# Softmax maxima negated bank by bank, and attention units passed in two rounds, in a four-layer macaron decoder

## The reference

```python
for l in range(4):
    h = h + 0.5 * swiglu(rms_norm(h), ffn1[l])          # 1024 -> 2816 -> 1024
    aq, ak, av, rq, rk, rv, rg = split(rms_norm(h) @ w_in[l])
    h = h + concat([attention(aq, ak, av, sinks[l]), retention(rq, rk, rv, rg)]) @ w_out[l]
    h = h + 0.5 * swiglu(rms_norm(h), ffn2[l])

def attention(q, k, v, sink):    # 8 query heads, 2 kv heads, 64 wide, window 128, blocks of 128
    s = q @ kk.T * 64 ** -0.5    # kk, vv: the block before and the block itself, 256 keys
    s = where(mask, s, -1e30)
    m = maximum(max(s), sink)
    p = exp(s - m)
    return (p / (sum(p) + exp(sink - m))) @ vv
```

## Time and profile before

| | us |
|---|---|
| median of 3 runs | 5002.9 (5000.14 to 5364.91) |
| the profiled execution, its own time | 4998.59 |
| span of its slowest core, and of all cores | 4997.0 (4987.1 to 4997.0) |
| TensorE matmul busy | 4824.5 (97%) |
| VectorE busy | 2432.0 (49%) |
| ScalarE busy | 1902.8 (38%) |
| GpSimd busy | 818.8 (16%) |
| mean granted TensorE clock | 0.991 of 2.4 GHz |

### The profile page before, as it was taken

How to read it: one execution, slowest core, us unless ns; L and a number is a source line. 1 busy time by engine, 2 the same in 40 slices (tenths; PEclk the granted TensorE clock), 3 DMA queues, 4 the chain that set the end, 5 groups by cost and what they waited for, 6 DMA issues and landing times.

```text
span 4997.0 us, 74942 instructions; the slowest of 8 cores (4987.1 to 4997.0 us)
## 1 busy us (share of the span) xinstructions
PE 4824.5 (97%) x24992; PEld 2229.8 (45%) x24992; DVE 2432.0 (49%) x4938; ACT 1902.8 (38%) x3615; POOL 818.8 (16%) x1150
## 2 busy tenths in 40 slices
PE   7998899999999999999999999999999999989898
PEld 3443444444444444444444444444444444444343
DVE  2265645454454545555454554545445454455532
ACT  2134533534234342433434343343432534263522
POOL 0121121210212112120210202102121210201121
PEclk9999999999999999999999999999999999999999
DMA  6444545464554545545445554545445354435255
GB/s 144 77 87 70 87 73 98 72 100 72 90 94 74 101 72 92 86 81 95 74 86 85 90 89 74 98 72 97 83 83 98 66 100 80 82 67 103 45 112 101
DMA packets 129032, 430.78 MB, mean 86 GB/s; under 512 B 14608, under 2 KB 14736, under 8 KB 128656
## 3 DMA queue, kind: packets, MB, share of 16 engines
q0 software_dynamic: 116640, 404.54, 47.5%
q1 hardware_dynamic: 12016, 21.45, 1.5%
HBM read 822.03 MB, written 8.39 MB: 166 GB/s over the span
## 4 chain that ended last, share of the span: by engine, by line
PE 88%; DVE 4%; ACT 4%; issue 2%; DMA 1%; POOL 1%; DVEq 0%; ACTq 0%; SPq 0%; POOLq 0%
PE pf L493 46%; PE pf L524 21%; PE pm L614 9%; PE pm L957 4%; PE pm L766 2%; DVE nF L427 1%; ACT scr L846 1%; PE pm L874 1%; PE pm L820 1%; PE pm L886 1%; ACT L846 1%; DVE pm L826 1%; PE pm L662 1%; DMA ringF<-w_gu 1%; DVE nM L427 0%
## 5 line engine op out<-in xcount | busy, mean ns | idle before, releaser
L493 PE MATMUL pf<-nF,ringF 128*128 128x512 bf16 x11264 | 2564.4, 382 | 15.6 <-DMA ringF<-w_gu 6.2
L493 PEld LDWEIGHTS pf<-nF,ringF 128*128 128x128 bf16 x11264 | 1080.2, 98 | 1290.8 <-issue 85.7
L524 PE MATMUL pf<-aT,ringF 128*128 128x512 bf16 x5456 | 1217.7, 380 | 16.5 <-DVE hT L528 15.3
L501 DVE TENSOR_TENSOR aT<-pf,sgt 128x512 bf16<-128x512 f32 x704 | 485.3, 690 | 1071.3 <-PE pf L493 807.3
L499 ACT ACTIVATE sgt<-pf 128x512 f32<-128x512 f32 x704 | 417.8, 595 | 1242.2 <-PE pf L493 1071.3
L524 PEld LDWEIGHTS pf<-aT,ringF 128*128 128x128 bf16 x5456 | 526.0, 98 | 650.4 <-issue 37.6
L528 DVE SCALAR_TENSOR_TENSOR hT<-pf,hT 128x512 f32<-128x512 f32 x496 | 336.3, 689 | 537.1 <-PE pf L524 472.5
L157 POOL DMA_DIRECT2D ringF<-w_gu x352 | 187.9, 534 | 2006.6 <-PE pf L493 887.8
L614 PE MATMUL pm<-ringM,nM 128*128 128x512 bf16 x2048 | 487.3, 380 | 4.2 <-DVE nM L427 3.7
L614 PEld LDWEIGHTS pm<-ringM,nM 128*128 128x128 bf16 x2048 | 200.1, 98 | 251.0 <-issue 15.2
L499 ACT ACT_TABLE_LOAD x161 | 206.6, 1283 | 242.5 <-PE pf L493 233.5
(11 more groups left out here) (114 smaller groups left out, 3546.5 us busy)
## 6 DMA issues: line engine op xcount, KB each, us to landing
ringF<-w_gu POOLq DMA_DIRECT2D x352, 512.0 KB, 5.4
ringF<-w_d POOLq DMA_DIRECT2D x124, 704.0 KB, 6.7
ringM<-w_r POOLq DMA_DIRECT2D x128, 512.0 KB, 6.5
ringM<-w_o POOLq DMA_DIRECT2D x128, 256.0 KB, 7.5
ringM<-w_aq POOLq DMA_DIRECT2D x32, 512.0 KB, 7.6
hT<-xT SPq DMA_DIRECT2D x16, 512.0 KB, 17.0
yT<-hT SPq DMA_DIRECT2D x16, 512.0 KB, 7.7
ringF<-w_d POOLq DMA_DIRECT2D x13, 352.0 KB, 4.9
```

The costliest lines, as they stand in the source:

```text
L493: A('pe', lambda e: e.matmul(PF[b][:], ringF_t[:, off:off + 128], nF[:, sub, k, :], start=(k == 0), stop=(k == KC - 1)), ringF.pages(key, ...
L501: A('dve', lambda e: e.tensor_tensor(out=aT[:, f, sub, :], in0=PF[b][:], in1=sg, op=ALU.mult), [('pf', b), ('sg', sub)], [('aT', f, sub)])
L524: A('pe', lambda e, b=b, a=a, f=f: e.matmul(PF[b][:], ringF_t[:, off + a:off + a + 128], aT[:, f, sub, :], start=(f == 0), stop=(f == HF - ...
```

## The change

The negated maximum is made for each score bank by itself, two columns each, directly behind that bank's maximum, and the exponentials of a bank wait for their own. In a round the transposes of unit `i-2` now stand ahead of the exponentials of unit `i-1`; the normalisation has a step of its own; `att_v` now takes unit `i-2` (before `i-3`) and shares a step with `att_s(i)`. A unit is done two rounds behind its scores and not three. The costs of the steps become 12, 12, 12, and the last projection's step goes from 8 to 14.

```diff
                     A('dve', lambda e, s3=s3, hg=hg: e.tensor_reduce(out=mx_t[:, pr, hg], in_=s3, axis=AX.X, op=ALU.max),
                       [('pm', g)], [('mx', pr, g)])
-                sl = slice(l * 8 + jp * 4, l * 8 + jp * 4 + 4)
-                A('dve', lambda e: e.scalar_tensor_tensor(out=nm_t[:, pr, :], in0=mx_t[:, pr, :], scalar=-0.125,
-                                                          in1=nsink[:, sl], op0=ALU.mult, op1=ALU.min),
-                  [('mx', pr, 0), ('mx', pr, 1), 'nsink'], [('nm', pr)])
+                    A('dve', lambda e, hg=hg, sg_=sg_: e.scalar_tensor_tensor(out=nm_t[:, pr, hg], in0=mx_t[:, pr, hg], scalar=-0.125,
+                                                                            in1=nsink[:, sg_], op0=ALU.mult, op1=ALU.min),
+                      [('mx', pr, g), 'nsink'], [('nm', pr, g)])
...
-                          [('pm', g), ('nm', pr)], [pg[g], ('den', pr, hx)])
+                          [('pm', g), ('nm', pr, g)], [pg[g], ('den', pr, hx)])
...
-            S_(8, avp, lambda: tr_out(2), lambda: tr_out(3))
+            S_(14, avp, lambda: tr_out(2), lambda: tr_out(3))
             NU = 2 * NB
             for i in range(NU + 3):
                 def r0(i=i):
-                    if 0 <= i - 3 < NU:
-                        att_v(i - 3)
-                    if 0 <= i - 1 < NU:
-                        att_e(i - 1)
-
-                def r1(i=i):
                     if 0 <= i - 2 < NU:
                         att_t(i - 2)
                     if 0 <= i - 1 < NU:
+                        att_e(i - 1)
+
+                def r1(i=i):
+                    if 0 <= i - 1 < NU:
                         att_n(i - 1)
 
                 def r2(i=i):
-                    if i < NU:
-                        att_s(i)
-                if i > 0:
+                    if 0 <= i - 2 < NU:
+                        att_v(i - 2)
+                    if 0 <= i - 0 < NU:
+                        att_s(i - 0)
+
+                if 1 <= i < NU + 2:
                     S_(12, r0)
-                if 0 < i < NU + 2:
-                    S_(10, r1)
-                if i < NU:
-                    S_(14, r2)
+                if 1 <= i < NU + 1:
+                    S_(12, r1)
+                if 0 <= i < NU + 2:
+                    S_(12, r2)
```

More of the change, by code:

```diff
@@ L822, in att_s @@
                           [('aq', j, qb), ('ak', qb), ('ak', qb + 1)], [('pm', g)])
+                sl = slice(l * 8 + jp * 4, l * 8 + jp * 4 + 4)
                 for g in range(2):
@@ L825, in att_s @@
                     mb = maskt[:, c0:256].unsqueeze(1).to_broadcast([128, 2, 256 - c0])
+                    hg = slice(2 * g, 2 * g + 2)
+                    sg_ = slice(l * 8 + jp * 4 + 2 * g, l * 8 + jp * 4 + 2 * g + 2)
                     A('dve', lambda e, s3=s3, mb=mb: e.tensor_tensor(out=s3, in0=s3, in1=mb, op=ALU.add),
                       [('pm', g), ('c', 'c_mask')], [('pm', g)])
-                    A('dve', lambda e, s3=s3, g=g: e.tensor_reduce(out=mx_t[:, pr, 2 * g:2 * g + 2], in_=s3, axis=AX.X, op=ALU.max),
+                    A('dve', lambda e, s3=s3, hg=hg: e.tensor_reduce(out=mx_t[:, pr, hg], in_=s3, axis=AX.X, op=ALU.max),
                       [('pm', g)], [('mx', pr, g)])
-                sl = slice(l * 8 + jp * 4, l * 8 + jp * 4 + 4)
-                A('dve', lambda e: e.scalar_tensor_tensor(out=nm_t[:, pr, :], in0=mx_t[:, pr, :], scalar=-0.125,
-                                                          in1=nsink[:, sl], op0=ALU.mult, op1=ALU.min),
-                  [('mx', pr, 0), ('mx', pr, 1), 'nsink'], [('nm', pr)])
+                    A('dve', lambda e, hg=hg, sg_=sg_: e.scalar_tensor_tensor(out=nm_t[:, pr, hg], in0=mx_t[:, pr, hg], scalar=-0.125,
+                                                                            in1=nsink[:, sg_], op0=ALU.mult, op1=ALU.min),
+                      [('mx', pr, g), 'nsink'], [('nm', pr, g)])
                 A('dve', lambda e: e.tensor_tensor(out=es_t[:, pr, :], in0=nm_t[:, pr, :], in1=sink[:, sl], op=ALU.add),
-                  [('nm', pr), ('c', 'c_sink')], [('es', pr)])
+                  [('nm', pr, 0), ('nm', pr, 1), ('c', 'c_sink')], [('es', pr)])
             def att_e(i):
@@ L919, in r0 @@
                 def r0(i=i):
-                    if 0 <= i - 3 < NU:
-                        att_v(i - 3)
+                    if 0 <= i - 2 < NU:
+                        att_t(i - 2)
                     if 0 <= i - 1 < NU:
@@ L925, in r1 @@
                 def r1(i=i):
-                    if 0 <= i - 2 < NU:
-                        att_t(i - 2)
                     if 0 <= i - 1 < NU:
```

## The result

Over 5 runs of each kernel the median went from 5002.9 to 4946.0 us (4942.28 at the lowest). The ratio, after to before, is 0.9883 with a 95% interval of 0.9869 to 0.9897; the profiled execution took 4944.91 us, where the one of before took 4998.59. So the time fell by 1.2%, which is within 2%, and 4946 stands beside a forecast of 4950.

What follows compares the result with a forecast made beforehand. Dense rounds were held bound by a loop through VectorE and ScalarE, sparse stages by TensorE's work. Rounds 29, pass ends 16.5, sparse 7 less 3 sum to 49.5 us off 4998.6: 4949, forecast 4950; case's own range 4933 to 4967.

Steps and rivals of the forecast that it cites:

- The loop in a dense round: Dense rounds, as long as a loop through VectorE and ScalarE, go from 8.8 and 9.57 us to 7.6 and 8.2.
- The fit of the copy in front: Dense rounds: the transposes' copy ends at about E+3.75, just as the exponentials may start, at E+3.75 or E+4.35.
- The rival in which the copy takes the gain back: Dense rounds: late transposes make each round pay their wait, rounds of 8.5 us, 4965 us in all; chance 0.17.
- The end of a pass: Dense passes, last scores to last values: 18.7 to 12.1 us in two, 2.4 less in the others; 16.5 taken together.
- The new wait on the last transposes: Dense stages: a new TensorE wait of 1 to 2 us before the last transposes (L876), released by VectorE.
- The clock: Last dense stage: mean granted clock rises above 0.96, half of the low-clock losses behind stalls being gone.
- The wait before scores: Dense stages: TensorE's idle time before the scores (L820) falls from 40 to about 25 us.
- Neither sign of being wrong: Wrong would be: TensorE waiting on L876 in each round, or new L493 waits on ScalarE's L499 above 6 us.
- The sparse passes: Sparse stages: 7 us saved on tile switches less 3 us lost to ScalarE's longer block.
- The term of adjacency: Sparse passes: values directly ahead of scores save one tile-size step of 0.08 to 0.10 us, 72 times, 7 us.
- The late Silu: Sparse stages: ScalarE's longer block delays the first Silu behind the transposes, 0.1 us about 30 times, 3 us lost (0 to 6).

Runs made afterwards that it cites:

- nm_only: The kernel before with only the negated maximum made bank by bank, rounds, order and step costs as before; 4960.0 us, 0.9924 of before.
- order_only: The changed kernel with one negated maximum for both banks, as before, its order and step costs kept; 4983.9 us, 0.9975 of before.
- dve_in_loop: The changed kernel with an unneeded 128x512 VectorE multiplication added in each unit directly ahead of the masks; 4958.0 us, 0.9920 of before.

## Why the prediction was right, step by step

**The loop in a dense round: right.** Four starts of scores on core 2 of after:

```profile
587.63 0.38 PE L820 MATMUL pm<-ak,AQ 64*128 64x256 bf16 x3 [0.84 <-ACT esk L852]
...
595.80 0.38 PE L820 MATMUL pm<-ak,AQ 64*128 64x256 bf16 x3 [0.85 <-ACT esk L852]
...
603.37 0.38 PE L820 MATMUL pm<-ak,AQ 64*128 64x256 bf16 x3 [0.85 <-ACT esk L852]
...
611.53 0.38 PE L820 MATMUL pm<-ak,AQ 64*128 64x256 bf16 x3 [0.84 <-ACT esk L852]
```

8.17, 7.57 and 8.16 us; forecast were 8.2 and 7.6. nm_only, order_only and dve_in_loop show that the mechanism is the one named. The seven distances of a pass, summed over the four dense passes on core 0, fell by 27.9 us, where 29 were forecast.

**The fit of the copy in front: right, but for 0.2 us.** VectorE and ScalarE in the round from 595.80:

```profile
599.17 0.16 DVE L833 SCALAR_TENSOR_TENSOR nmx<-mx,nsink 128x2 f32<-128x2 f32 x1
...
600.88 0.16 DVE L833 SCALAR_TENSOR_TENSOR nmx<-mx,nsink 128x2 f32<-128x2 f32 x1
```

```profile
598.55 1.02 ACT L880 ACTIVATE scr<-pm 128x1024 bf16<-128x1024 bf16 x1 [0.89 <-PE pm L876]
599.59 1.28 ACT L848 ACT_TABLE_LOAD   x1
600.89 0.47 ACT L848 ACTIVATE scr<-pm,nmx 128x256 bf16<-128x256 f32 x1
```

The table load starts as the copy ends, at 599.59. Normalisation started at 595.85 (E), so this is E+3.74, where E+3.75 was forecast. The first negated maximum started at 599.17 and was ready 0.26 us before the load; by the 0.24 us that lie between the two where nothing is in front the load could have started at 599.41. So in this shorter round the copy ends last and holds the exponentials for 0.18 us; in the longer one they start at E+4.35, as forecast, by the maximum. The second negated maximum was ready at 601.04, during the first exponential. The rival in which the copy takes the gain back fell for this reason: it takes 0.18 us in every other round.

**The end of a pass: the mechanism right, the size too small.** From the last scores (620.87) to the last values (632.63) it is 11.8 us in the first stage's second pass, where 18.7 stood before and 12.1 were forecast; in its first pass, which ends among down groups, 12.0 (434.65 to 446.66) and before 14.8. The new wait on the last transposes came as said, by VectorE, at 1.5 us a stage. Over the four dense passes of core 0 the ends fell from 66.7 to 47.6 us in sum, 19.1 us, where the forecast took 16.5 and at most 18: it kept back 1.5 us for a low clock behind the waits, and took 2.4 for the passes that end among down groups, which gave 2.8 and 2.3. (Its 12.1 is a slip, too: the terms written there add up to 12.0.) Rounds and ends had 45.5 us in the sum and give 47.0 on core 0; the dense stages show 46.1. That the whole fits better than its parts is luck.

**The clock: right in direction.** 0.98 against "above 0.96". Of 24.0 us at the low clock 8.8 are gone. nm_only, with its 11.1, loses less than after, so it isn't the order that brings this gain.

**The wait before scores: right in size.** 27.7 us, forecast about 25. Neither sign of being wrong came: TensorE waits on L876 at the ends of passes and not in each round, and its waits of L493 on the Silu (L499) are 3.7 us in the whole trace, 3.0 before.

**The sparse passes: the sign right, the term too small.** 4 us in the sum, 9.5 measured in 12 passes. The term of adjacency had 7 (72 steps of 0.10) and was right: 6.7 to 7.6, by the count ahead of scores. The late Silu had 3 (about 30 places of 0.1) and cost 5.4 to 5.9: fewer places, 24 in 12 passes, but 0.17 to 0.47 us at each, 0.28 at the one shown. Both lie within their bounds. What the sum left out is the rest of the order, 7.8 to 8.6 us in 12 passes, for which it had no term. With it the total was missed by 6.1 us (55.6 on equal cores against 49.5), of which 0.6 belong to the dense stages. That 4950 came within 4 us of 4946 owes something to the Silu, whose extra cost hides a third of what was left out.

## What to carry to other kernels

Where an engine that is half idle stands in a loop, work out the loop's length by latency, engine by engine, and cut it where a consumer waits for two halves and needs one. Before moving an instruction in an engine's queue, work out each loop that the new order closes, not only the one it opens: the copy behind the exponentials cost 8.3 us in a dense stage with the values two groups behind the transposes, and with the values one group behind made the whole kernel slower than before. When a round is latency-bound, giving it more independent work can be worth as much as shortening it, until the work that it was taken from runs short.

## What the runs showed of the hardware

- Values (64 columns wide) and scores (64 rows) in a row cost 0.35 and 0.32 us from start to start (434.30 to 434.97 in after), the same as each has among full matmuls; the only price seen for the change from full matmuls is 0.09 to 0.11 us ahead of them.
- Waits of 1.13 and 0.85 us before a round's scores were followed by 8 matmuls of 512 columns in 3.53 us, at 1.2 GHz, in one round of the earlier trace rows, and by the same in 1.90 us, at 2.4 GHz, in the round before. The first of the two waits in the slower round:

```profile
4468.22 0.27 PE L820 MATMUL pm<-ak,AQ 64*128 64x256 bf16 x1 [1.13 <-ACT scr L846]
```

- ScalarE's first exponential starts 1.29 to 1.30 us behind its table load's start, in every dense round read (4465.56 to 4466.85 before, 599.59 to 600.89 after).
